# A decoder layer on one core: the o projection, its norms and the residual by rows of tokens

## The chip, the cores and the metric

The kernel runs on one core of a Trainium2 chip, in one launch. The metric is the device time of an execution in microseconds. The kernel before takes 1654.36 us, the median of three runs (1653.92 to 1654.64). Engines: PE is TensorE (PEld its weight loads), DVE is VectorE, ACT is ScalarE, POOL is GpSimd, SP is SyncE, whose queue issues nearly all DMAs.

## The reference

One decoder layer in float32, width 1024, for a prompt of 1024 tokens and, with its own convolution state, for 8 single sample tokens. The part that matters here:

```
z  = rms_norm(x, mix_pre_g) @ w_in            # split into u, v, b, c, x_in, r_a, r_b
v  = layer_norm(gelu(v));  y_a = (gelu(u) * spatial_mix(v)) @ w_a_out
y_b = (b * short_conv(c * x_in)) @ w_b_out
h  = sigmoid(r_a) * y_a + sigmoid(r_b) * y_b
o  = h @ w_o
x1 = x + rms_norm(o, mix_post_g)
f  = (silu(n @ w_gate) * (n @ w_up)) @ w_down,  n = rms_norm(x1, ffn_pre_g)
y  = x1 + rms_norm(f, ffn_post_g)
```

rms_norm divides a token's row by the root of its mean square and multiplies with a gain per column. The FFN is 2816 wide.

## The kernel before

**Numbers and layout.** Each float32 operand is split into a rounded high part and the rest (hi, lo), and a product is three matmuls: hi hi, hi lo, lo hi (`three`, L379). Most of the kernel keeps activations turned: channels lie on the partitions, tokens along the free axis. The 1032 tokens are four chunks (b, gg) of 258: 256 of the prompt and 2 samples. A matmul then has a 128x128 block of weights as stationary operand and 258 tokens moving. `tp` holds the operand's eight slots, hi and lo; `g` a stage's result; `ring_hi`/`ring_lo` seven prepared weight pieces; `stage0`, `stage1` the weights as they were loaded, 1 MB each; `ps` the eight banks of PSUM. Weight block b is loaded by SP (`load`, L711), ScalarE writes its hi parts (`hi`, L1112), GpSimd subtracts for the lo parts (`rest`, L953). Most blocks use a scheme of seven products in place of eight, with sums of quarters of weights (`sums`) and of activations made by VectorE; `QORDER` lists the plain blocks that use eight (`half`, L470).

**Stage of v (L386 to L462).** Nine tiles of tokens, the 8 samples first. Rows are loaded (`x_load`), ScalarE squares them with a sum, VectorE makes the root in eleven small instructions (`rsqrt`, L1516) and scales. TensorE turns eight blocks of the normalised rows (`turn_norm`), and eight of the raw rows (`turn_raw`); ScalarE copies the raw ones out and stores them in `xt_dram` (`keep`, L1089). v itself is computed with tokens as stationary operand and 512 columns of w_v moving, 48 matmuls a tile (`v_tile`). The transposes of tile i+2 stand behind the matmuls of tile i.

**The o stage (L583 to L606, L1321 to L1342, L1935 to L1977).** For each chunk, eight blocks m of 128 output columns: 24 matmuls with w_o's 128x128 blocks stationary and the chunk's 258 tokens moving. ScalarE evicts with the gain (L1326) and squares (L1332), GpSimd adds the squares, and a matmul with ones sums them over the partitions (`norm_sum`, L572) so that every partition has each token's sum. VectorE makes the root over 128x258 and scales (`x1`), adds the residual `xts`, loaded from `xt_dram`; ScalarE squares, VectorE adds, ones sum again (`second_norm`), and `x1_norm` scales into `g`. x1 is stored in `x1_dram`. `f_split` (ACT) and `f_rest` (DVE) then make hi and lo in `tp`. The first blocks of gate and up (`B_F`, `B_UP0`) run as four half runs on one half of the tokens each, plain, so that they can begin when chunks 0 and 1 are there. The next block pair uses seven products and needs the quarters' sums (`ft_total`, `ft_rest`).

**The end (L641 to L693, L1487, L2178).** y is computed turned. For each of 18 units (128 tokens by 512 columns) TensorE turns four blocks of f and four of x1, ScalarE copies x1 out of PSUM, VectorE scales and adds (`y_unit`), and SP stores rows.

**Order.** Each engine's order is written out by hand; engines meet through semaphores. What stands behind a waiting instruction in an engine's queue waits with it. w_o is loaded in columns, 128 of them a piece (`o_load`).

Of the kernel before, what the change touches and what calls it, by code (L numbers as in the profile page):

```python
# [7 lines left out]
D = 1024  # L8
# [22 lines left out]
B_UP0 = B_F + 1  # L31
B_D = B_F + 2 * J
# [31 lines left out]
STAGE = [b % 2 if b <= B_F else (0 if b == B_UP0 else (b + 1) % 2) for b in range(B_END)]  # L64
# [14 lines left out]
def places(b):  # L79
    return [0, 1, 2, 3] if b in QORDER else list(range(7)) if B_UP0 < b < B_D else TURNED  # L80


def freed(b, pos):
    place = places(b)[pos]
    if b == B_F + 2:
        return used(B_F, place) if place < 4 else done(LAST_RUN[B_UP0], 3)
# [25 lines left out]
O_LOADS = [0, 2, 1, 3, 4, 6, 5, 7]  # L112
O_ORDER = [O_LOADS] * 3 + [[0, 2, 4, 6, 1, 3, 5, 7]]
O_SLOT = {1: 5, 3: 7, 5: 4, 7: 6}
O_RING = {2: 4, 4: 0, 6: 2}
PARTS = [slice(0, 3), slice(3, 6), slice(6, 8)]
P_POST, P_PRE, P_OUT, P_CONV, P_LN = 0, KT, 2 * KT, 3 * KT, 6 * KT
P_ROWS = 7 * KT

def build(nc, x_prompt, x_sample, state_conv, mix_pre_g, mix_post_g, w_in, sgu_ln_g, sgu_ln_b, w_s,  # L120
# [7 lines left out]
    xt_dram = nc.dram_tensor("xt_dram", [4, 128, KT, 256], f32, kind="Internal").ap()  # L128
    xs_dram = nc.dram_tensor("xs_dram", [128, 4, KT, 2], f32, kind="Internal").ap()
    x1_dram = nc.dram_tensor("x1_dram", [4, 128, KT, CS], f32, kind="Internal").ap()  # L130
# [6 lines left out]
    with ctx:  # L137
# [36 lines left out]
        xt_odd = at("xt_odd", stage_at[1], [128, KT, CS])  # L174
        q = at("q", q_at, [128, 4, 2, CS])
        xt_even = at("xt_even", q_at, [128, KT, CS])
        xts = [(xt_even, xt_odd)[c % 2] for c in range(4)]
        inv_early, work_early = (at(n, ring_at + (6 + 7 * i) * 2048, [128, CS]) for i, n in enumerate(("inv_early", "work_early")))
# [5 lines left out]
        x_norm = at("x_norm", ring_at + 4096 * 2, [128, D])  # L184
        x_save = at("x_save", ring_at + 4096 * 3, [128, D])
# [12 lines left out]
        xs_raw = at("xs_raw", g_at + KT * D * 4, [128, 4, KT, 2])  # L198
        tail_out = s_bc[0:(2 + NS) * KT, 1].rearrange("p a c -> p (a c)")[:, 0:128]
        o_sum, o_sq0, o_sq1, x1_sum, base_t, root = s_a[:, 0], s_a[:, 1], s_b[:, 0], s_b[:, 1], s_c[:, 0], s_c[:, 1]  # L200
        invs = [inv_early[:, :]] * 3 + [q[:, 2, 1]]
        works = [work_early[:, :]] * 3 + [q[:, 3, 1]]
# [6 lines left out]
        xs = at("xs", hist_at, [128, 4, KT, 2])  # L209
# [4 lines left out]
        x1_smp = at("x1_smp", tail_at, [128, KT, NS])  # L214
# [39 lines left out]
        def norm_bank(n, c):  # L254
            return 6 + n if c < 3 else (7, 5)[n]

        x1_late = [at(f"x1_late{n}", stage_at[1] + n * 4096, [128, D]) for n in range(2)]
        x1_rows = [piece(5, u // 2, u % 2) for u in range(4)] + [t[:, :] for t in x1_late] + [piece(6, part, 0) for part in range(2)]
        y_rows = [piece((4, 0, 1, 2)[u // 2], u % 2, 0) for u in range(8)] + [piece(7, 0, 0)]
# [7 lines left out]
        def y_banks(v):  # L267
            return (4, 2, 0)[v % 3], (5, 3, 1)[v % 3]
# [21 lines left out]
        def w_ring(b, pos, kp=MP):  # L290
            if b != B_UP0:
                hi, lo = ring_hi[:, places(b)[pos]], ring_lo[:, places(b)[pos]]
            elif pos < 3:
                hi, lo = ring_hi[:, 4 + pos], ring_lo[:, 4 + pos]
            else:
                hi, lo = (tp[:, 3, part, 0].rearrange("p k c -> p (k c)")[:, 0:512] for part in range(2))
            return tuple(w[:, 0:128 * kp].rearrange("p (k c) -> p k c", c=128) for w in (hi, lo))

        def raw_part(b, pos, kp=MP):
            n = STAGE[b]  # L300
            k_odd, m_odd = divmod(pos, 2)[::-1] if b in QORDER else {0: (0, 0), 2: (1, 0), 6: (1, 1)}[pos]
            return stage[n][:, k_odd:2 * kp:2, 128 * m_odd:128 * m_odd + 128]

# [21 lines left out]
        raw_turned, norm_turned = sem("raw_turned"), sem("norm_turned")  # L325
        raw_copied, xt_saved = sem("raw_copied"), sem("xt_saved")
# [7 lines left out]
        stage_in = [sem("stage_in0"), sem("stage_in1")]  # L334
        s_sum, w_hi, w_lo = sem("s_sum"), sem("w_hi"), sem("w_lo")
# [6 lines left out]
        xs_in, xs_spread, xs_saved = sem("xs_in"), sem("xs_spread"), sem("xs_saved")  # L342
# [17 lines left out]
        o_full, o_copied, o_acc = sem("o_full"), sem("o_copied"), sem("o_acc")  # L360
        n_sum, n_sqrt, n_base, inv_ready = sem("n_sum"), sem("n_sqrt"), sem("n_base"), sem("inv_ready")
        xt_in, x1_saved = [sem("xt_in0"), sem("xt_in1")], sem("x1_saved")
        x1_done, x1_sq, x1_total, x1n_ready = sem("x1_done"), sem("x1_sq"), sem("x1_total"), sem("x1n_ready")
# [5 lines left out]
        x1_in, y_turned, y_done = [sem("x1_in0"), sem("x1_in1")], sem("y_turned"), sem("y_done")  # L369
        y_out, y_packed, x_turned, x1_copied = sem("y_out"), sem("y_packed"), sem("x_turned"), sem("x1_copied")  # L370
# [7 lines left out]
        def _(pe):  # L378
# [7 lines left out]
            def turn_raw(i):  # L386
                rows = rows_of(V_TILES[i])
                pe.wait_ge(x_in[i % 2], 16 * (i // 2 + 1))
                if i:
                    pe.wait_ge(raw_copied, i)  # L390
                for k in range(KT):
                    ins = pe.transpose(ps[:, 4 + k // 4, 128 * (k % 4):128 * (k % 4) + rows],  # L392
                                       x_rows[i % 2][0:rows, 128 * k:128 * k + 128], ident[0:rows, 0:rows])
                ins.then_inc(raw_turned, 1)

            def turn_norm(i):
                rows = rows_of(V_TILES[i])
                pe.wait_ge(x_scaled, i + 1)
                if i:
                    pe.wait_ge(xn_lo_done, i)  # L400
                for k in range(KT):
                    ins = pe.transpose(ps[:, 6 + k // 4, 128 * (k % 4):128 * (k % 4) + rows],  # L402
                                       x_norm[0:rows, 128 * k:128 * k + 128], ident[0:rows, 0:rows])
                ins.then_inc(norm_turned, 1)

            def v_tile(i):
# [4 lines left out]
                for k in range(KT):  # L411
                    if i == 0:
                        if k == 3:
                            turn_norm(1)
                        pe.wait_ge(wv_lo, k + 1)
# [10 lines left out]
            def turn_consts():  # L426
                pe.wait_ge(raw_copied, 9)
                pe.wait_ge(xn_lo_done, 9)
                pe.wait_ge(row_in, 16 * 7)
# [142 lines left out]
            def norm_sum(n, c, what):  # L572
                pe.matmul(ps[:, norm_bank(n, c), 0:CS], ones[:, :], what, start=True, stop=True).then_inc(n_sum, 1)

            def first_norm(c):
                pe.wait_ge(o_acc, (KT - 1) * (c + 1))
                norm_sum(0, c, o_sum)

            def second_norm(c):
                pe.wait_ge(x1_total, c + 1)  # L580
                norm_sum(1, c, x1_sum)
# [1663 lines left out]
```

## Time and profile before

| | us |
|---|---|
| median of three runs | 1654.36 |
| the profiled execution | 1651.66 |
| its span | 1649.9 |
| TensorE busy in it | 1616.9 |
| VectorE busy | 991.3 |
| ScalarE busy | 549.2 |
| GpSimd busy | 682.4 |

The span is the time from the first to the last recorded event of the profiled execution; the rest of its 1651.66 us lies around it. Busy times overlap between engines. Matmuls are pipelined, so a record's length is more than the distance to the next one. A timeline row merges like instructions in a row (x8), and a bracket at its end says how long the engine stood idle before it and what ended that.

### The profile page before, as it was taken

The numbers are of one execution on the slowest core, as the hardware profiler recorded it, in microseconds if no ns is written. First come the engines' busy times: TensorE is split into PE (matmuls) and PEld (weight loads), VectorE is DVE, ScalarE is ACT, GpSimd is POOL, SyncE is SP. The second block draws the span as 40 slices with busy tenths as digits, with TensorE's granted clock in tenths as the row PEclk, the third lists the DMA queues.
The fourth block names the chain that finished last, engine by engine and source line by source line (L and its number), as shares of the span: only waits on it lengthen the run. The fifth ranks groups of instructions, "written<-read, shape, count | busy, mean of one in ns | idle before, by whom it ended". The sixth has DMA issues, their size and how long they took to land.

```text
span 1649.9 us, 31035 instructions
## 1 busy us (share of the span) xinstructions
PE 1616.9 (98%) x12966; PEld 1586.1 (96%) x12966; DVE 991.3 (60%) x1409; ACT 549.2 (33%) x864; POOL 682.4 (41%) x495
## 2 busy tenths in 40 slices
PE   8999999999999999999999899999999999999998
PEld 5889999999999999999999899999999999999998
DVE  7657667587583334224428986444444447595976
ACT  5322332222223334212243543322223234342544
POOL 1001444444444443323442435444444443555392
PEclk9999999999999999999999999999999999999999
DMA  6302011320313335522332323222222324333433
GB/s 236 126 28 77 27 52 33 97 78 33 97 59 104 104 109 187 174 94 74 90 90 81 124 79 103 78 78 77 78 78 77 97 72 142 100 126 102 130 103 129
DMA packets 148494, 157.75 MB, mean 96 GB/s; under 512 B 6076, under 2 KB 136004, under 8 KB 147844
## 3 DMA queue, kind: packets, MB, share of 16 engines
q1 hardware_dynamic: 139732, 151.51, 28.6%
q10 hardware_dynamic: 8624, 4.27, 0.9%
q8 instruction: 103, 1.69, 0.4%
q14 instruction: 35, 0.29, 0.1%
HBM read 118.70 MB, written 37.09 MB: 94 GB/s over the span
## 4 chain that ended last, share of the span: by engine, by line
PE 86%; DVE 8%; issue 2%; DMA 1%; ACT 1%; SPq 0%; POOL 0%; DVEq 0%; ACTq 0%
PE ps L383 84%; DVE tp L2036 1%; PE ps L466 1%; DVE tp_f L2046 1%; DVE tp L1969 1%; DVE g L1961 1%; DMA gv<-in_w_in 1%; DMA stage<-in_w_gate 0%; DVE tp L2003 0%; PE ps L402 0%; PE ps L667 0%; PE ps L392 0%; DMA tp_f<-hid_dram 0%; PE ps L673 0%; DVE g L1951 0%
## 5 line engine op out<-in xcount | busy, mean ns | idle before, releaser
L383 PE MATMUL ps<-tp,ring_hi 128*128 128x258 f32 x7676 | 1253.4, 284 | 13.3 <-DVE tp L2036 6.4
L383 PEld LDWEIGHTS ps<-tp,ring_hi 128*128 128x128 f32 x7676 | 1069.7, 190 | 15.2 <-issue 13.1
L383 PE MATMUL ps<-tp,ring_lo 128*128 128x258 f32 x3838 | 796.1, 283 | 0.0
L383 PEld LDWEIGHTS ps<-tp,ring_lo 128*128 128x128 f32 x3838 | 606.7, 191 | 0.0
L962 POOL TENSOR_TENSOR ring_lo<-stage,ring_hi 128x512 fp32r<-128x512 f32 (+1 forms) x212 | 317.6, 1504 | 600.9 <-ACT ring_hi L1128 600.7
L962 POOL TENSOR_TENSOR ring_lo<-ring_f,ring_hi 128x512 fp32r<-128x512 f32 (+1 forms) x204 | 294.9, 1458 | 237.2 <-DVE ring_f L1623 109.6
L1128 ACT ACTIVATE ring_hi<-ring_f 128x512 fp32r<-128x512 f32 (+1 forms) x204 | 127.4, 626 | 484.0 <-DVE ring_f L1623 169.7
L1128 ACT ACTIVATE ring_hi<-stage 128x512 fp32r<-128x512 f32 (+1 forms) x212 | 128.7, 618 | 203.9 <-PE ps L383 145.6
L1620 DVE TENSOR_TENSOR ring_f<-stage 128x512 f32<-128x512 f32 (+1 forms) x51 | 40.4, 793 | 186.4 <-PE ps L383 117.8
L383 PE MATMUL ps<-wv_hi_t,tp 128*128 128x512 f32 x256 | 71.8, 397 | 0.0
L1641 DVE TENSOR_TENSOR s_a<-ps,s_a 128x516 f32<-128x516 f32 (+1 forms) x52 | 35.6, 684 | 49.2 <-PE ps L383 48.1
L2036 DVE TENSOR_TENSOR tp<-tp_f,tp 128x2064 fp32r<-128x2064 f32 (+1 forms) x24 | 58.2, 2428 | 1.2 <-ACT tp L1395 1.2
L383 PEld LDWEIGHTS ps<-wv_hi_t,tp 128*128 128x128 f32 x256 | 47.5, 188 | 10.6
L383 PE MATMUL ps<-tp 128*128 128x258 f32 x432 | 56.1, 288 | 0.0
L1139 ACT ACTIVATE s_a<-ps 128x516 f32<-128x516 f32 (+1 forms) x52 | 30.7, 589 | 72.3 <-PE ps L383 57.1
L383 PEld LDWEIGHTS ps<-tp 128*128 128x128 f32 x432 | 54.2, 193 | 0.4
L1652 DVE TENSOR_TENSOR s_a<-ps,s_a 128x516 f32<-128x516 f32 (+1 forms) x52 | 35.5, 682 | 31.8 <-PE ps L383 31.6
L1628 DVE TENSOR_TENSOR ring_f<-stage,ring_f 128x512 f32<-128x512 f32 (+1 forms) x51 | 53.5, 1048 | 0.0
L1892 DVE TENSOR_TENSOR g<-ps,q 128x516 f32<-128x516 f32 x16 | 11.1, 695 | 68.9 <-PE ps L383 61.0
L1395 ACT ACTIVATE tp<-tp_f 128x2064 fp32r<-128x2064 f32 (+1 forms) x24 | 42.6, 1780 | 20.5 <-DMA tp_f<-hid_dram 19.1
L2068 DVE TENSOR_TENSOR hq<-hq,q 128x516 f32<-128x516 f32 x40 | 44.9, 1123 | 2.2
L1911 DVE TENSOR_TENSOR s_bc<-ps,q 128x516 f32<-128x516 f32 x16 | 11.1, 695 | 49.9 <-PE ps L383 47.0
(235 smaller groups left out, 1306.3 us busy)
## 6 DMA issues: line engine op xcount, KB each, us to landing
stage<-in_w_in SPq DMA_DIRECT2D x24, 1024.0 KB, 5.8
stage<-in_w_gate SPq DMA_DIRECT2D x11, 1024.0 KB, 6.0
stage<-in_w_up SPq DMA_DIRECT2D x11, 1024.0 KB, 5.4
hid_dram<-hq SPq DMA_DIRECT2D x40, 258.0 KB, 3.1
tp_f<-hid_dram SPq DMA_DIRECT2D x20, 516.0 KB, 5.1
stage<-in_w_down SPq DMA_DIRECT2D x8, 1024.0 KB, 5.7
ob_dram<-q SPq DMA_DIRECT2D x16, 258.0 KB, 2.9
ra_dram<-q SPq DMA_DIRECT2D x16, 258.0 KB, 2.1
```

The source lines that it names most:

```text
L383: ins = pe.matmul(o, w, xc, start=first and n == 0, stop=last and n == 2)
L466: ins = pe.matmul(ps[:, 2 * r + n // 4, 128 * (n % 4):128 * (n % 4) + 128], gv[:, n, 128 * m:128 * m + 128], ws_t[:, 128 * m:128 * m + 128 ...
L962: pool.tensor_tensor(lo, src, hi.bitcast(f32), SUB).then_inc(w_lo, 1)
L1128: act.activation(w_ring(b, p, kp)[0], src, ACT.Copy).then_inc(w_hi, 1)
L1139: act.activation(s_a[:, gs], reg(Z, gs), ACT.Copy).then_inc(s1_done, 1)
L1395: act.activation(slot(s, 0, both, ks), slot_f(2 if s == 7 else s, 1, both, ks), ACT.Copy).then_inc(t_hi, 1)
L1620: ins = dve.tensor_tensor(out, a21, a22, ADD)
L1628: ins = dve.tensor_tensor(out, a12, ring(ring_f, b, 3, kp), SUB)
L1641: dve.tensor_tensor(s_a[:, gs], reg(X, gs), s_a[:, gs], ADD).then_inc(u1_done, 1)
L1652: dve.tensor_tensor(s_a[:, gs], reg(Z, gs), s_a[:, gs], ADD).then_inc(u2_done, 1)
L2036: dve.tensor_tensor(slot(s, 1, both, ks), slot_f(2 if s == 7 else s, 1, both, ks), slot_v(s, 0, both, ks), SUB).then_inc(t_lo, 1)
L2068: dve.tensor_tensor(hq[:, n], hq[:, n], q[:, n], MUL).then_inc(hid_ready, 1)
```

## The change

In the stage of v the raw transposes, their copies and `xt_dram` go. x_norm has two buffers and the normalised rows of tile i+1 are turned in the middle of tile i's matmuls, in two pairs of banks in turn.

The o projection takes tokens as stationary operand: for each of nine tiles (128 tokens, or the 8 samples, packed by GpSimd into `smp_hi`/`smp_lo`) the product goes to two banks, with 512 columns of w_o's rows moving. w_o is loaded by rows. Tiles 0 and 1 run interleaved, row block by row block. Each token's sum of squares is then along the free axis: ScalarE squares with a sum, VectorE makes the root on one column and scales straight from PSUM into the one buffer `x1n_rows`, adds the residual rows `res` (loaded from the input, two buffers), ScalarE squares again, VectorE scales into `x1n_rows`, TensorE turns eight blocks, ScalarE copies them to `g` (`x1n_keep`). x1 is stored by rows.

The first gate and up blocks get homes of their own in `tp` (`RAW_SLOT`), loaded after the last residual rows. At the end x1 is loaded straight into `y_rows`; a unit is four transposes of f, and every third unit is scaled by ScalarE and added by GpSimd.

```diff
+O_TILES = [2, 3, 8, 0, 1, 6, 7, 4, 5]
+O_BANK = [4, 2, 0] * 3
 # TensorE, stage of v
-            turn_raw(0)
             turn_norm(0)
-            turn_raw(1)
             for i in range(9):
-                v_tile(i)
-                if i + 2 < 9:
-                    turn_raw(i + 2)
-                    turn_norm(i + 2)
+                v_tile(i)              # turn_norm(i + 1) at its k == 4 (3 where i == 0)
 # TensorE, o stage
+            def o_part(i, j, k):
+                t, (a, kp) = O_TILES[i], (k % 2, k // 2)
+                if i < 2:
+                    pe.wait_ge(o_lo, j + 1)
...
+                outs = [ps[0:rows_of(t), O_BANK[i] + n, :] for n in range(2)]
+                w_h, w_l = ([w[:, 512 * n:512 * n + 512] for n in range(2)] for w in (w_o_hi[k], w_o_lo[k]))
+                ins = three(outs, x_h, x_l, w_h, w_l, j == 0, j == KT - 1)
+            def turn_x1n(i):
+                pe.wait_ge(x1n_ready, i + 1)
+                if i:
+                    pe.wait_ge(x1n_kept, i)
+                for k in range(KT):
+                    ins = pe.transpose(ps[:, x1n_banks(i)[k // 4], ...], x1n_rows[...], ident[...])
+                ins.then_inc(x1n_turned, 1)
+            for j, k in enumerate(O_LOADS):
+                o_part(0, j, k)
+                o_part(1, j, k)
+            for i in range(2, 9):
+                if i == 2:
+                    pe.wait_ge(o_packed, 8)
...
+                if i >= 3:
+                    pe.wait_ge(o_scaled, i - 2)
+                for j, k in enumerate(O_LOADS):
+                    o_part(i, j, k)
+                    if j == (KT - 1 if i == 2 else KT - 3):
+                        turn_x1n(i - 2)
+            turn_x1n(7)
             for i in range(4):         # gate on the first half of the tokens
...
                 half(r, i, PLAIN_BANK[i], lambda q: (f_lo, (3, 1, 4, 2)[q]))
+            turn_x1n(8)
 # VectorE
+            def x1(i):
...
+                y = o_root(i, i, o_sq)
+                if i == 0:
+                    dve.wait_ge(post_in, 16)
+                else:
+                    dve.wait_ge(x1n_turned, i)
+                dve.scalar_tensor_tensor(normed, o_rows, y, post_gain[0:rows], MUL, MUL).then_inc(o_scaled, 1)
+                dve.wait_ge(o_scaled, i + 1)
+                dve.wait_ge(res_in[i % 2], 16 * (i // 2 + 1))
+                dve.tensor_tensor(res[i % 2][0:rows, :], res[i % 2][0:rows, :], x1n_rows[0:rows, :], ADD).then_inc(x1_done, 1)
+            def x1_norm(i):
...
+                y = o_root(i, 9 + i, x1_sq)
+                dve.scalar_tensor_tensor(dst, src, y, pre2_gain[0:rows], MUL, MUL).then_inc(x1n_ready, 1)
+            for i in range(9):
+                x1(i)
+                if i == 5:
+                    f_rest(0)
+                elif i == 7:
+                    f_rest(1)
+                x1_norm(i)
 # ScalarE, from the seventh tile on (x1_square, x1n_keep and o_square before it likewise)
+            o_square(7)
+            prepare(B_F)
+            x1_square(7)
+            x1n_keep(6)
+            o_square(8)
+            x1n_keep(7)
+            prepare(B_UP0, 0, 3)
+            f_split(2)
+            x1_square(8)
+            silu_plain(r, 0)
 # SP
+            for i in range(7):
+                x1_save(i)
+                res_load(i + 2)
             load(B_F)
             load(B_UP0)
+            x1_save(7)
             load(B_F + 2)
+            x1_save(8)
 # GpSimd, behind w_o's low parts and the packing of the samples
-            (spread_samples, add_square and rest(B_F, ...) in turn)
+            prepare(B_F)
             prepare(B_UP0)
 # The end: y_bank(v) = (4, 2, 0, 5, 3, 1)[v % 6]; v % 3 == 0 on ScalarE and GpSimd
+            for v in range(18):        # VectorE
+                if v == 7:
+                    y_root_of(1)
+                    y_root_of(2)
+                if v % 3:
+                    y_unit(v)
```

## Rows read from the trace of the kernel before

**Rows 1.** The page: span, busy time, the chain's shares by engine.
```profile
span 1649.9 us, 31035 instructions
...
PE 1616.9 (98%) x12966; PEld 1586.1 (96%) x12966; DVE 991.3 (60%) x1409; ACT 549.2 (33%) x864; POOL 682.4 (41%) x495
...
PE 86%; DVE 8%; issue 2%; DMA 1%; ACT 1%; SPq 0%; POOL 0%; DVEq 0%; ACTq 0%
```

**Rows 2.** TensorE's waits: who waited for whom: total us, times, longest.
```profile
PE ps L573 <- DVE s_bc L1953: 5.0, 4, 3.3
...
PE ps L402 <- DVE x_norm L1530: 5.0, 2, 3.4
```

**Rows 3.** The chain in order of time: start us, length us, what.
```profile
40.62 11.09 PE ps L383 x48
...
51.71 0.87 PE ps L392 x8
...
211.11 277.75 PE ps L383 x2304
```

**Rows 4.** Timeline, all engines, 0 to 30: start, length, engine, line, idle before.
```profile
13.57 1.00 PE L383 MATMUL ps<-wv_lo_t,smp_hi 128*8 128x512 f32 x2
...
22.08 1.22 DVE L1542 TENSOR_TENSOR tp<-ps,tp 128x1024 fp32r<-128x1024 f32 x1
...
23.22 0.14 DVE L1527 TENSOR_SCALAR small<-small 128x1 f32<-128x1 f32 x1
...
23.59 0.63 PE L383 MATMUL ps<-wv_hi_t,smp_lo 128*8 128x512 f32 x2
...
25.33 1.28 DVE L1530 SCALAR_TENSOR_TENSOR x_norm<-x_rows,small,pre_gain 128x1024 f32<-128x1024 f32 x1
...
27.51 0.71 PE L383 MATMUL ps<-wv_hi_t,tp 128*128 128x512 f32 x2
```

**Rows 5.** Timeline 100 to 145, and a group of the page.
```profile
120.14 5.04 POOL L962 TENSOR_TENSOR ring_lo<-stage,ring_hi 128x512 fp32r<-128x512 f32 x4 [87.08 <-ACT ring_hi L1128]
...
121.49 1.21 DVE L1519 TENSOR_TENSOR small<-small 128x1 f32<-128x1 f32 x1
...
L1892 DVE TENSOR_TENSOR g<-ps,q 128x516 f32<-128x516 f32 x16 | 11.1, 695 | 68.9 <-PE ps L383 61.0
```

**Rows 6.** TensorE's timeline from 815 to 1003.
```profile
826.08 3.15 PE L383 MATMUL ps<-tp,stage_r 128*128 128x258 f32 x24 [1.09 <-POOL tp L973]
...
922.25 1.21 PE L573 MATMUL ps<-s_bc,ones 128*128 128x258 f32 x2 [3.30 <-DVE s_bc L1953]
...
922.90 4.48 PE L383 MATMUL ps<-tp 128*128 128x258 f32 x24
...
978.34 0.64 PE L383 MATMUL ps<-tp,ring_hi 128*128 128x258 f32 x4
...
994.80 0.72 PE L383 MATMUL ps<-tp,ring_hi 128*128 128x258 f32 x4 [1.82 <-DVE q L1635]
```

**Rows 7.** Timelines: ScalarE at 52, VectorE in the o stage.
```profile
52.67 1.02 ACT L1105 ACTIVATE x_save<-ps 128x1024 f32<-128x1024 f32 x1
...
922.12 3.88 DVE L1969 TENSOR_TENSOR tp<-g,tp 128x1032 fp32r<-128x1032 f32 x2
...
948.04 2.37 DVE L1969 TENSOR_TENSOR tp<-g,tp 128x1032 fp32r<-128x1032 f32 x2
```

**Rows 8.** The chain at 905; DMA issues: KB each, median us to landing.
```profile
905.54 8.08 DMA stage<-in_w_gate
...
stage<-in_w_gate SPq DMA_DIRECT2D x11, 1024.0 KB, 6.0
```

**Rows 9.** The end: VectorE's and GpSimd's timelines, then the last stretch by engine.
```profile
1635.69 11.61 DVE L2183 SCALAR_TENSOR_TENSOR tp_f<-ps,small,tp_f 128x512 f32<-128x512 f32 x14
...
1630.86 0.19 POOL L1039 COPY sum_smp<-q 128x8 f32<-128x8 f32 x1
...
1645.00:1649.90 4.90, 1.32 (x13) 1.08 (x10) 2.06 (x3) 1.20 (x2) 0.00 (x0) 0.94 0.74 293
```

More of the change, by code:

```diff
@@ L252, in ysq @@
             return q[:, 2 + n]
[L254 to L259, printed above, removed]
+        x1_late = [at(f"x1_late{n}", stage_at[0] + n * 4096, [128, D]) for n in range(2)]
+        y_rows = [piece(5, u // 2, u % 2) for u in range(4)] + [t[:, :] for t in x1_late] \
+            + [piece(6, part, 0) for part in range(2)] + [piece(7, 0, 0)]
         SAMPLES = 8
@@ L1148, in _ @@
                 wv_split(k)
-            keep(1)
+            norm_split(1)
+            square(2)
             for i in range(9):
+                if 0 < i < 8:
+                    norm_split(i + 1)
                 if 0 < i < 7:
@@ new lines, in x1n_keep @@
+            def x1n_keep(i):
+                t = O_TILES[i]
+                act.wait_ge(x1n_turned, i + 1)
+                first, second = x1n_banks(i)
+                if t == 8:
+                    rows = bank_pair(first, NS).rearrange("p k (g b i) -> p b g k i", g=2, b=2)
+                    for b in range(2):
+                        for gg in range(2):
+                            ins = act.activation(g[:, :, b, gg, 256:CS], rows[:, b, gg], ACT.Copy)
+                else:
+                    b, gg, off = home(t)
+                    dst = g[:, :, b, gg, off:off + 128]
+                    if second == first + 1:
+                        ins = act.activation(dst, bank_pair(first), ACT.Copy)
+                    else:
+                        for n, bank in enumerate((first, second)):
+                            ins = act.activation(dst[:, 4 * n:4 * n + 4], ps[:, bank, :].rearrange("p (k c) -> p k c", c=128), ACT.Copy)
+                ins.then_inc(x1n_kept, 1)
@@ L1955, in x1_norm, with o_root @@
-            def x1_norm(c):
-                b, gg = O_CHUNKS[c]
-                dve.tensor_copy(x1_smp[:, :, 4 * gg + 2 * b:4 * gg + 2 * b + 2], xts[c][:, :, 256:CS])
-                o_rsqrt(1, c)
-                for h in PARTS:
-                    for m in range(h.start, h.stop):
-                        ins = dve.scalar_tensor_tensor(g[:, m, b, gg], xts[c][:, m], par[:, P_PRE + m:P_PRE + m + 1], invs[c], MUL, MUL)
-                    ins.then_inc(x1n_ready, 1)
+            def o_root(i, col, ready):
+                rows = rows_of(O_TILES[i])
+                a, y, w = (small[0:rows, 20 + n:21 + n] for n in range(3))
+                dve.wait_ge(ready, i + 1)
+                link(dve.tensor_scalar(a, small[0:rows, col:col + 1], 1.0 / D, EPS, MUL, ADD))
+                rsqrt(y, a, w)
+                return y
@@ L1964, in f_rest @@
+            def x1_norm(i):
+                rows = rows_of(O_TILES[i])
+                quarters = (t[0:rows, :].rearrange("p (n c) -> p n c", n=4) for t in (x1n_rows, res[i % 2]))
+                dst, src = quarters
+                y = o_root(i, 9 + i, x1_sq)
+                if i == 0:
+                    dve.wait_ge(pre2_in, 16)
+                dve.scalar_tensor_tensor(dst, src, y, pre2_gain[0:rows], MUL, MUL).then_inc(x1n_ready, 1)
             def f_rest(c):
```

590 lines of the change are left out of this document (241 added, 349 removed).

## The prediction

> **What bounds the kernel now.** I began with the page: TensorE is busy 98% of the span, its chain share is 86%, and no other engine is above 60% [rows 1]. So a change counts by three things: TensorE work added or removed, waits opened or closed, and what lies behind the last matmul. The waits come next [rows 2]: little idle time, much of it before the sums over partitions that the change removes. Then the shapes. A tile of v, 48 matmuls of 512 columns, takes 11.09 us in the chain, 0.231 us each, and eight transposes take 0.87 us; 2304 matmuls of 258 columns take 277.75 us, 0.1206 each [rows 3]. I then read three places as timelines: the start [rows 4], the o stage [rows 6], and the end [rows 9].
>
> The sum is made against the profiled execution: 1651.66 us, 1649.9 of it span. The median of the runs is 2.7 us higher, at 1654.36; the time that I give is the difference added to that median.
>
> **Stage of v: raw transposes and their copies go.** TensorE first. Each tile of tokens loses one group of eight transposes. Before the second tile TensorE now stands until the rows for the third are normalised (VectorE 25.33 to 26.61) and starts its matmuls at 27.51, though the first tile ended at 24.0 (23.59 and two matmuls) [rows 4]. In the new order these transposes lie in the middle of the second tile, 5.5 us after its start, and their rows are ready by then. The tile itself can start at 24.0, since the low part of its own rows is there at 23.3 (22.08 and 1.22) [rows 4]. That is 3.5 us earlier, and the third tile's own transposes (0.87) are paid inside: 2.6. Six more tiles lose 0.87 each, 5.2. Together **-7.8**. What is late next? Per tile VectorE has 2.1 us of a norm's root (23.22 to 25.33), 1.3 of scaling, 1.2 of low part and some 4.6 of layer norm, 9.3 in all, under a new period of 11.1 + 0.87 = 12.0; so TensorE still sets the pace. Removed ScalarE copies, stores of xt, and SP's wait on the raw transposes cost nothing now, being beside matmuls. Less activity at the very start may leave the first tile longer at the lower clock (1.2 GHz: two 512-column matmuls last 1.00 there against 0.71 later [rows 4]), but its last part waits for loads anyway: 0 to +0.8. Bounds: -8.3 to -7.0.
>
> **o projection: TensorE work.** Removed: 768 matmuls at 0.1206 = 92.6, and 8 sums over partitions, 16 matmul records of 258 columns, 1.9. Added: 8 tiles of 48 matmuls of 512 columns, and the ninth, 8 samples as stationary operand, which costs as much as a full tile, as two such matmuls in the stage of v (0.63) do beside two of a full tile (0.71) [rows 4]: 9 x 11.09 = 99.8. Transposes of the normalised rows: 8 x 0.87 and a small one, 7.5. The four half runs of gate and up that follow, 384 matmuls, are 46.2 in both. Work after: 99.8 + 7.5 + 46.2 = 153.5. The same stretch of before lasts from 826.08 to 978.34, 152.3 with its waits, and the first up-weighted product after it has one more wait of 1.8, behind a crowded VectorE [rows 6]: 154.1. So if no wait were left, the stage would be level: -0.6. All that the transposes saved there would be the waits.
>
> **o projection: the waits that come.** The first two tiles run interleaved with the arriving rows of w_o, 2.8 us a row block against 2.4 of GpSimd for its low part, as now. From the third on, a tile's chain runs: turn of the tile before ends (x1n_rows is one buffer), scale from PSUM 1.3, add 1.2 (as the 128x1024 low part), square on ScalarE 1.1 (its 128x1024 copy is 1.02), root 2.1, scale 1.3, turn [rows 4, 7]: 7.4 with hand-overs, 8.6 in the turn where two f_rest lie beside the square. The turns are 12.0 apart, so this is hidden by 2 us or more, about 1 at the first two.
>
> The last full tile is different. Its turn is issued right behind the ninth tile's matmuls, only 2.8 us after the turn before. Against that stand: scale to 1.4, add to 2.6, two f_rest (2.4 free, 3.9 beside GpSimd [rows 7]) to 6.4; ScalarE meanwhile has the four gate-weight copies, queued ahead of the square, which end about 5 (the load, 6.0 us [rows 8], is issued after the last residual load), so the square ends about 6.4 too; root 2.1 to 8.5; scale 1.3 to 9.8; hand-over 0.1. With free ports TensorE waits 9.9 - 2.8 = 7.1. But GpSimd then subtracts the four gate weights. Beside just such a block of four (5.04 us) the small VectorE instructions of a root took 1.21 us each instead of 0.19 pitch, four in the block, of which one stands in the rows [rows 5]. Instructions with an operand in PSUM keep their time: 695 ns mean for 516 columns [rows 5]. I take it that two of this root's eleven are caught, +2.0, and 0.2 for the square: wait **9.3**, bounds 7.1 and 12.
>
> The Trainium skill has a rule here, in "SBUF — State Buffer", section "SBUF: two separate sides": a VectorE instruction with two SBUF inputs and a GpSimd one exclude each other for the whole instruction. By that rule every one of the eleven root instructions could wait a full GpSimd one until the four are done, some 5 us and not 2.2; the wait would be 12, the end of my bound.
>
> Then the clock. After 3.30 idle at 922.25 the granted clock shows the lower level, and 24 matmuls span 4.48 against 2.9 to 3.0 warm: 1.5 lost [rows 6]. After a longer wait I take 2.0, bounds 1.5 and 3.4. Behind the wait all is covered: the ninth turn lies after 11.6 us of gate products, while its chain (scale, add, square behind f_split, root, scale) is some 9 to 10; up's first half hides the last f_rest. The sums of quarters for the first seven-product run are finished before the last half run, so the 1.8 of before should not return. SP's order (saves, residual loads, then weights) has 3 to 5 us to spare at each tile. Stage: -0.6 + 9.3 + 2.0 = **+10.7**, bounds +8.0 and +14.8.
>
> **The end.** Now every unit of 512 columns is eight transposes, 0.87 us, and VectorE's 14 last units take 11.61 (1635.69 to 1647.30) [rows 9]. After: four transposes a unit, every third unit on ScalarE and GpSimd, two of three on VectorE at 0.75 (PSUM operand, so not slowed). The first units can be scaled from about 1629.2 as before the samples' sum. GpSimd starts its adds at 1631.05; VectorE does four units to 1632.2, then both roots, partly beside two adds, to 1635.5; eight units at 0.75 to 1641.5; GpSimd's last four adds at 1.3 from 1635.5 end 1640.7. Computing thus ends 5.8 earlier. But three output tiles, 1.5 MB, become ready within the last 1.5 us; the last stretch shows 293 GB/s at a share of 0.74 [rows 9], 396 at full share, so 4 us of transfer plus 1.8 fixed: end at about 1645.5. **-4.5**, bounds -6.0 and -2.5.
>
> Elsewhere (u to gates, the other up and gate products, down) the edits only rename slots and stages: 0, within 0.5.
>
> **Sum.** -7.8 + 10.7 - 4.5 = -1.6: 1650.1 for the profiled execution, **1652.8** on the median.
>
> **Rivals.** Bound between "same" and the others is 0.2%, 3.3 us, about what a measurement can tell: below 1651.1 faster, above 1657.7 slower.
> First, the turn's wait is short: roots escape GpSimd, idle costs little clock (7.1 + 1.5 - 0.6 = 8.0), and the last stores are not held by transfer (-5.8): -7.8 + 8.0 - 5.8 = -5.6, 1648.8. For it: the 695 ns of PSUM instructions, and that the weights' block may start after the root. Against: f_rest at 3.88 beside GpSimd [rows 7], in this very stretch. With the wait of the turn gone wholly it would be near 1642.
> Second, slower: the gate weights land late. Gate and up are issued back to back, 2 MB; if their packets share the engines, gate lands after 12 us and not 6. Its four copies stand in ScalarE's queue ahead of the square of the last tile, so the square, root and turn slip by 6: wait 15.3, clock 3: stage +17.7, sum -7.8 + 17.7 - 4.5 = +5.4, 1659.8. It decides from a landing about 7 us after issue. For: 8.08 us at 905.54, behind another megabyte. Against: the median of 6.0 [rows 8], and that nothing large is issued ahead of gate here.
> Third, the shapes do not do what I read: rows of w_o as 512-column operand from the ring cost more than w_v's, or the single buffer of rows makes a wait in each of six tiles of 1 us or more. Then +6 and up, 1659 or more. Little speaks for it: 0.231 holds for all v tiles, the 8-row one too.
>
> **Numbers.** Forecast and its neighbourhood within 0.2%: 0.45. First rival with what lies beyond: 0.36. Second: 0.12, third: 0.07. Range: 8 in 10 from 1646.5 to 1659.0, which holds the bounds of the three parts taken mostly together (all low -6.3, all high +5.3). Faster 0.36, same 0.45, slower 0.19.
>
> **What would show it.** Second tile of v starts near 24.0 and tiles come every 12.0; the o stage has nine blocks of 11.1; one TensorE wait of 7 to 12 us before the transposes of the last full tile, on VectorE's scaling, with half clock behind it; no wait of 1.8 in the first seven-product run; last transposes near 1640 in old time. Wrong if waits stand at several turns, if that one is under 5, or if the end gains less than 2.5.

## The result: 2.6 us slower, 0.15%

Over 20 executions each the changed kernel takes 1654.97 us in the median (1652.88 to 1657.45), the kernel before 1652.36 (1651.57 to 1654.66): ratio 1.0015, 95% interval 1.0008 to 1.0021. The forecast was a difference of -1.6 us, 1652.8; the three runs that its base was taken from stood 2.0 us above the median of the twenty. The profiled execution of the changed kernel took 1653.63 us, 1651.8 of it span. Its page, line by line against [rows 1]:

```profile
span 1651.8 us, 30181 instructions
...
PE 1611.5 (98%) x12542; PEld 1557.3 (94%) x12542; DVE 971.5 (59%) x1512; ACT 524.8 (32%) x801; POOL 661.0 (40%) x477
...
q8 instruction: 100, 1.64, 0.4%
```

TensorE's waits (who waited for whom: total us, times, longest), against [rows 2]. The waits before the sums over partitions, 5.0 us in four, are gone; one of 9.4 has come. Two small ones on VectorE's `q`, at 489 and 423, were not there before:

```profile
PE ps L584 <- DVE x1n_rows L1937: 9.4, 1, 9.4
PE ps L397 <- DVE x_norm L1521: 7.4, 1, 7.4
PE ps L388 <- DVE tp L2009: 7.4, 3, 3.4
...
PE ps L553 <- DVE q L1647: 1.3, 1, 1.3
```

Both kernels cut at the same points of the program (end of the v stage, first product of the o stage, the first product after the first wait of the down stage, that after the third, end). First before, then after; columns: stretch, its length, busy time of each engine with its instructions, granted clock, DMA share, GB/s:

```profile
0.00:198.65 198.65, 188.97 (x1170) 162.59 (x1170) 137.72 (x315) 66.85 (x89) 30.88 (x31) 1.00 0.30 97
198.65:826.08 627.43, 626.19 (x5193) 625.83 (x5194) 331.11 (x481) 172.51 (x276) 265.87 (x185) 1.00 0.29 93
826.08:1395.89 569.81, 559.38 (x4601) 557.05 (x4601) 330.59 (x411) 197.44 (x336) 252.02 (x189) 1.00 0.29 91
1395.89:1552.17 156.28, 151.48 (x1243) 151.13 (x1243) 117.82 (x107) 60.40 (x74) 75.34 (x49) 0.99 0.38 121
1552.17:1649.90 97.73, 90.89 (x762) 89.49 (x762) 74.04 (x98) 52.04 (x91) 58.34 (x42) 1.00 0.31 98
```

```profile
0.00:190.49 190.49, 180.10 (x1098) 153.84 (x1098) 138.17 (x315) 60.04 (x79) 30.74 (x31) 1.00 0.24 79
190.49:820.29 629.80, 626.68 (x5193) 625.96 (x5194) 329.65 (x481) 172.43 (x276) 264.63 (x185) 1.00 0.29 93
820.29:1401.45 581.16, 569.54 (x4320) 544.62 (x4321) 315.74 (x520) 186.27 (x295) 224.08 (x165) 0.99 0.28 90
1401.45:1558.36 156.91, 151.71 (x1242) 151.18 (x1243) 117.95 (x107) 60.25 (x74) 75.73 (x49) 0.99 0.38 120
1558.36:1651.80 93.44, 83.47 (x690) 81.69 (x690) 69.95 (x92) 45.78 (x79) 65.80 (x48) 0.99 0.27 103
```

Read by differences: -8.16 in the v stage, **+2.37 in a stretch with the same 5193 matmuls in both**, +11.35 from the o stage to the first wait of down (0.61 of it that wait: 2.24 for 1.63), +0.63 within down, -4.29 at the end. Together +1.9, as the spans.

The one large wait is the forecast's, link by link. The chain of the changed kernel (start us, length, what):

```profile
923.10 0.89 PE ps L584 x8
...
924.09 1.29 DVE x1n_rows L1925
...
925.41 1.22 DVE res L1928
926.63 3.36 DVE tp L1944 x2
...
930.28 0.89 DVE small L1510
...
931.20 1.20 DVE small L1511
...
934.80 1.30 DVE x1n_rows L1937
...
936.14 1.97 PE ps L584 x8
```

TensorE was through with the ninth tile at 926.8 and stood until 936.1. The turn then took 1.97 us instead of 0.87, at the lower clock.

### The profile page after: what moved, and what is told of

Same layout as the page of the kernel before. It is cut to its first block, busy times and chain, and to the rows that moved or that the text cites. A ratio compares the mean times of both kernels' runs of the same rounds, so it can differ in the third digit from the quotient of the medians.

```text
span 1651.8 us, 30181 instructions
## 1 busy us (share of the span) xinstructions
PE 1611.5 (98%) x12542; PEld 1557.3 (94%) x12542; DVE 971.5 (59%) x1512; ACT 524.8 (32%) x801; POOL 661.0 (40%) x477
## 4 chain that ended last, share of the span: by engine, by line
PE 90%; DVE 5%; issue 2%; DMA 1%; ACT 0%; POOL 0%; DVEq 0%; SPq 0%; POOLq 0%; ACTq 0%
PE ps L388 88%; DVE tp L2009 1%; PE ps L455 1%; DVE tp_f L2019 1%; PE ps L584 1%; DMA stage<-in_w_down 0%; DMA stage<-in_w_in 0%; PE ps L397 0%; DMA tp_f<-hid_dram 0%; ACT tp L1381 0%; DVE g L2102 0%; DVE tp L1944 0%; DVE tp_f L2158 0%; POOL ring_lo L959 0%; DVE s_a L1642 0%
## 5 line engine op out<-in xcount | busy, mean ns | idle before, releaser
L388 PE MATMUL ps<-tp,ring_hi 128*128 128x258 f32 x7388 | 1200.0, 284 | 11.3 <-DVE tp L2009 7.4
L388 PEld LDWEIGHTS ps<-tp,ring_hi 128*128 128x128 f32 x7388 | 1024.8, 190 | 12.7 <-issue 12.7
L388 PE MATMUL ps<-tp,ring_lo 128*128 128x258 f32 x3694 | 755.2, 283 | 0.0
L388 PEld LDWEIGHTS ps<-tp,ring_lo 128*128 128x128 f32 x3694 | 579.4, 191 | 0.0
L959 POOL TENSOR_TENSOR ring_lo<-stage,ring_hi 128x512 fp32r<-128x512 f32 (+1 forms) x205 | 304.4, 1492 | 570.2 <-ACT ring_hi L1088 570.1
L1088 ACT ACTIVATE ring_hi<-stage 128x512 fp32r<-128x512 f32 (+1 forms) x205 | 124.5, 617 | 199.3 <-PE ps L388 139.6
L388 PE MATMUL ps<-tp 128*128 128x512 f32 (+1 forms) x384 | 72.0, 340 | 0.0
L388 PEld LDWEIGHTS ps<-tp 128*128 128x128 f32 x384 | 59.7, 191 | 8.5
L959 POOL TENSOR_TENSOR tp<-tp_f,tp 128x512 fp32r<-128x512 f32 x4 | 6.5, 1645 | 94.2 <-ACT tp L1088 94.2
```

The source lines that it names most:

```text
L388: ins = pe.matmul(o, w, xc, start=first and n == 0, stop=last and n == 2)
L959: pool.tensor_tensor(lo, src, hi.bitcast(f32), SUB).then_inc(w_lo, 1)
L1088: act.activation(w_ring(b, p, kp)[0], src, ACT.Copy).then_inc(w_hi, 1)
```

## Experiments

Times are medians in us; the ratio is to the kernel before on the same chip in the same job, with its 95% interval. The kernel before took 1653.96 us in the job of e1 to e4, 1653.33 in that of e5 to e8, 1653.12 for e9 to e11 and 1653.22 for e12 to e14, so times of different jobs are compared by their ratios. The last five columns are the stretches above in us, each from one profiled execution:

```
                              time     ratio   interval          to end v  same work  o to down  down    end
before                        1652.36  1                         198.65    627.43     569.81     156.28  97.73
after                         1654.97  1.0015  1.0008 to 1.0021  190.49    629.80     581.16     156.91  93.44
e1 rest early                 1655.07  1.0005  0.9996 to 1.0014  191.16    630.10     581.12     156.88  93.94
e2 e1 + two row buffers       1646.47  0.9956  0.9944 to 0.9968  191.71    629.26     572.90     155.20  93.63
e3 v stage only               1649.98  0.9976  0.9964 to 0.9987  191.22    630.02     572.48     156.47  97.81
e4 end only                   1648.43  0.9965  0.9953 to 0.9977  198.61    628.08     569.85     156.04  93.12
e5 e2 + square first          1647.10  0.9962  0.9950 to 0.9975  191.02    629.20     573.42     156.60  93.86
e6 e1 + square first          1654.75  1.0009  1.0000 to 1.0018  191.45    629.08     581.58     158.33  93.56
e7 e3 + 128 waits on TensorE  1654.31  1.0011  1.0002 to 1.0021  197.04    627.58     572.03     155.12  97.83
e8 e5 + 128 waits             1652.35  0.9992  0.9984 to 1.0001  198.69    628.01     574.96     156.20  93.64
e9 e5 + GpSimd later          1651.72  0.9992  0.9983 to 1.0000  190.62    630.20     577.34     157.36  93.78
e10 e6 + GpSimd later         1656.43  1.0024  1.0015 to 1.0033  190.77    630.80     581.51     158.66  93.56
e11 e9 + 54 small turns       1648.45  0.9973  0.9964 to 0.9982  191.36    627.48     576.44     156.25  93.57
e12 e11 + GpSimd twice later  1644.71  0.9950  0.9936 to 0.9965  191.29    627.56     573.32     156.16  93.87
e13 before + 51 small turns   1658.86  1.0035  1.0022 to 1.0048  199.51    629.55     572.21     157.68  98.85
e14 e3 + 54 small turns       1648.67  0.9972  0.9959 to 0.9984  191.37    627.98     571.74     158.82  98.79
```

### The parts alone: e3 and e4

e3 is the kernel before with `turn_raw` and `keep` gone, two homes for `x_norm`, and the v stage's order of the changed kernel; e4 is the kernel before with the changed end. Both leave out part of what the layer computes: e3 reads its residual from other elements of the input, e4 adds x where x1 belongs, with the same number of bytes. e7 and e14 below are built on e3.

```diff
+                sp.dma_start(xts[c][:, :, 0:256], x_prompt[0, 256 * (2 * b + gg):256 * (2 * b + gg) + 256, :]
+                             .rearrange("(p r) (j c) -> p (r j) c", r=2, c=256))
...
+                    dst, src = y_rows[u], x_prompt[0, 256 * (2 * gg + b) + cols.start:...]
```

> The kernel before with the v stage of the changed one alone: no raw rows turned, copied or saved; the residual of the o stage is loaded with the same number of bytes from other elements of the input (so the residual is left out of what is computed). Theory V (8.1 us gained in the v stage and kept): 1643.9 to 1644.9, that is 7.5 to 8.5 us under the kernel before. Rival L (the earlier v stage makes loads of the next stages land late for TensorE, as the two waits of 0.6 and 1.3 us in the changed kernel's profile at 423 and 489 us): 5.0 to 6.5 us under it, with these two waits in its profile.

> The kernel before with the end of the changed one alone: no turns of the residual, a third of the units scaled by ScalarE and added by GpSimd; the residual added is x instead of x1 (same bytes, from the input). Theory E (the end gains 4.3 us as the two profiles stand to each other, and nothing else moves): 1647.6 to 1648.6, that is 3.8 to 4.8 us under the kernel before. Rival D (the end gains 4.3 us but the new end's loads, or other chances of transfers, cost the 1.3 us that the down stage lost in the changed kernel): 2.5 to 3.5 us under it, with waits of over 2 and over 3.4 us in the down stage.

e3: rival L, and more. The v stage ends 7.4 us earlier, but the kernel gains only 4.0 (0.24%, interval 0.13 to 0.36%). Both waits are there:

```profile
PE ps L549 <- DVE q L1616: 1.3, 1, 1.3
PE ps L384 <- DVE q L1594: 0.9, 2, 0.7
```

So they came with the v stage, not with the o stage. Then 2.7 us more went between 821 and the down stage, of which 0.8 is a longer first wait of down and most of the rest lower clock (last section). e4: 5.8 us under before by the ratio (0.35%, interval 0.23 to 0.47%), 5.5 by the medians, 4.6 of them in the end stretch of its profile; theory E, a little above it. The only loss elsewhere is 0.65 us in the equal stretch, with a wait of 0.79 us at 495 that before's profile does not have, though TensorE's instructions up to there are the same in both: so much comes and goes between executions.

### The large wait, one arm at a time: e1, e6, e10, and with two buffers e2, e5, e9

```diff
 e1:             if i == 7: f_rest(1)      # before x1(i), was behind it
 e6 = e1 and     x1_square(7)              # before prepare(B_F) on ScalarE, was behind it
 e10 = e6 and    pool.wait_ge(x1n_ready, 8)  # before prepare(B_F) on GpSimd
 e2 = e1 and     x1n_rows in two homes by turns: sb_at, and q[:, :, 0, 0:256]
                 dve.wait_ge(x1n_turned, i - 1)   # was i
 e5 = e2 and     x1_square(7) first
 e9 = e5 and     pool.wait_ge(x1n_ready, 8)
```

> The changed kernel with the two subtractions of the second column block (VectorE, 3.4 us in all) set before the scaling of the eighth tile instead of between its two norms. Theory W (the 9.4 us wait of TensorE is the length of VectorE's chain after the turn of the seventh tile, 12.0 us from 924.1 to 936.1): the wait falls by 3.4 to 6.0 us, and some of the slow small operations beside GpSimd move too; 3.4 to 5 us faster than the changed kernel, so 1650.0 to 1651.6 on its median of 1654.97. Rival R (the chain is set by what GpSimd and the landing of the gate weights do at 925 to 934): the small operations wait on, the wait stays above 8 us, and the gain is under 1.5 us.

> As e1_rest_early, and the normed rows have two homes by turns (the second in the part of q that is free then), so that VectorE can scale a tile while TensorE still has to turn the one before. Theory W: the chain of the eighth tile starts some 9 us earlier, the wait of 9.4 us goes to under 2, the clock does not fall, and the kernel is 9 to 12 us faster than the changed one: 1643 to 1646, 0.4 to 0.6% under the kernel before. Rival R (something else than the one row buffer holds the tile back, VectorE's own 10 us of work per tile or the gate weights): a wait of 4 us or more stays before the turn of the eighth tile or at the first product of the gate stage, and the time is 1648 or more.

e1 missed: the wait went from 9.4 to 8.8 only. Rival R described it. The 3.4 us of subtractions were one of two arms side by side; the other was ScalarE, whose square stood behind the split of weights that landed late. VectorE's timeline of e1:

```profile
926.47 1.22 DVE L1928 TENSOR_TENSOR res<-res,x1n_rows 128x1024 f32<-128x1024 f32 x1
931.40 0.15 DVE L1912 TENSOR_SCALAR small<-small 128x1 f32<-128x1 f32 x1 [3.71 <-ACT g L1279]
```

e2 was right in kind and a little short of its numbers (1646.47 for 1643 to 1646, a wait of 2.3 us for under 2): no lower clock after the wait, and 8.2 us less than e1 from o to down. The second buffer without the early subtractions was not run.

> As e1_rest_early (one row buffer), and ScalarE squares the eighth tile's sum before it splits the gate weights. In e1 the two subtractions were gone from the chain, but VectorE then sat 3.7 us for that square, which stood behind weights that landed at 928.1; the wait only went from 9.4 to 8.8. If these are two arms of one wait, taking both away must shorten it by 3 us or more: a wait of 5 to 6.5 us, and 3 to 4.5 us less than the changed kernel, 1650.5 to 1652. If the one row buffer alone set the 9 us, it stays above 8 and the time within 1 us of the changed kernel's 1654.97.

> As e2_two_rows, and ScalarE squares the eighth tile's residual sum before it splits the gate weights instead of behind that (in e2 the square waited until 923.3, and VectorE 3.2 us for it). Theory S (the rest of the wait, 2.3 us before the turn at 929.8, is ScalarE's order): the turn waits under 0.5 us and the kernel is 1.5 to 2.5 us faster than e2_two_rows, 1644 to 1645. Rival G (the split gate weights are late then): a wait of 1 us or more appears before the first products of the gate stage, and the time stays within 1 us of e2_two_rows.

Both missed in the same way: 8.6 and 2.7 us of wait stayed although both arms were gone. GpSimd's four subtractions now started at once beside the root. VectorE's timeline of e5:

```profile
922.38 0.16 DVE L1514 SCALAR_TENSOR_TENSOR small<-small 128x1 f32<-128x1 f32 x1
922.57 1.13 DVE L1515 SCALAR_TENSOR_TENSOR small<-small 128x1 f32<-128x1 f32 x1
923.74 1.23 DVE L1513 TENSOR_TENSOR small<-small 128x1 f32<-128x1 f32 x1
925.01 1.21 DVE L1514 SCALAR_TENSOR_TENSOR small<-small 128x1 f32<-128x1 f32 x1
926.25 1.22 DVE L1515 SCALAR_TENSOR_TENSOR small<-small 128x1 f32<-128x1 f32 x1
927.50 0.16 DVE L1513 TENSOR_TENSOR small<-small 128x1 f32<-128x1 f32 x1
```

GpSimd worked from 922.38 to 927.45: four instructions, four small ones slowed, 4.1 us.

> As e6_rest_and_square_early (one row buffer), and GpSimd waits for the scaling of the eighth tile. In e6 the wait was 8.6 us, with four small operations at 1.12 to 1.21 us beside GpSimd. Theory P: the wait falls by 4.1 us to about 4.5 us, and the time by 3.5 to 5 us, to 1650 to 1651.5 (the changed kernel 1654.97). If the row buffer alone set it, 8.6 us stay. Rival Q as for e9: the subtractions, started 4 us later against their use, cost over 1.5 us at the first products of the gate stage.

> As e5_two_rows_square_first, and GpSimd starts its four subtractions of the gate weights (5.07 us) only when the eighth tile is scaled. Theory P (what is left of the wait is the slowing of VectorE beside GpSimd: in e5 four small operations of the chain took 1.13 to 1.23 us instead of 0.16 while GpSimd was at work from 922.4 to 927.5, 4.1 us in all): these four take 0.16 us each, the scaling ends at about 925, the wait of 2.7 us before the turn at 929.4 is gone, and the kernel is 2 to 3 us faster than e5's 1647.1. Rival Q (GpSimd's work is only moved in front of the gate stage): a wait of over 1.5 us before its first products, and no gain over 1 us.

The mechanism held to a tenth: e10's wait before the eighth tile's turn is 8.61 - 4.06 = 4.55, e9's is gone. The gain did not come: by the ratios e10 is 2.5 us slower than e6 and e9 5.0 slower than e5, where gains of 3.5 to 5 and of 2 to 3 were expected. GpSimd's block ran into the ninth tile's root instead, and that tile's turn waited 3.5 us in e10 and 3.8 in e9, after which the clock in e9 was at half for 5 us. In e9 (who waited for whom, 821 to 960):

```profile
PE ps L587 <- DVE x1n_even L1943: 3.8, 1, 3.8
```

So the 9.4 us are a chain with three movable arms (subtractions, ScalarE's order, GpSimd's block) on a single row buffer; taking arms away one by one gave nothing (from o to down 581.1 to 581.6 us in e1, e6 and e10), the second buffer gave 8.2 (e2 against e1, e5 against e6).

### The late loads: e7, e8, e11 to e14

What delays the unchanged stretch is one load of w_in. VectorE's timeline, first before, then after:

```profile
428.53 0.69 DVE L1620 TENSOR_TENSOR ring_f<-stage 128x512 f32<-128x512 f32 x1 [6.78 <-DMA stage<-in_w_in]
```

```profile
422.04 0.69 DVE L1610 TENSOR_TENSOR ring_f<-stage 128x512 f32<-128x512 f32 x1 [8.41 <-DMA stage<-in_w_in]
```

Issued at 422.34 and 414.21, it landed 6.1 and 7.7 us later. The transfers of the changed kernel from 419 to 421 show what is in it:

```profile
q1 hardware_dynamic: 688, 0.69, 101.5%
q8 instruction: 1, 0.02, 3.0%
```

One packet of 16 KB, for 3% of 16 engines in 2 us, that is 1 us of one engine. The page has 103 such packets before and 100 after:

```profile
q8 instruction: 103, 1.69, 0.4%
```

TensorE's 12966 matmuls and as many weight loads, with its waits, are some 26400 instructions, 256 for each of the 103 packets, and the changed kernel's 12542 by the same count some 25600 for its 100; in steady work they come 15.4 us apart (128 matmuls of 0.1206). The change takes 72 transposes, with their weight loads 144 instructions, out of the v stage, and so moves every later fetch against every later load. In before they fall at about 415 and 431, on both sides of this load, in after at 419.

The Trainium skill, "Perfetto Trace Analysis", section "The 4-stage abstract model", has an instruction at 64 bytes, by which 256 make the 16 KB; the trace agrees. The Trainium skill, "Trainium Architecture — The Big Picture", section "The software stack", has the instruction streams brought to the engines when the program is loaded; here that is not the whole of it: the 103 packets come all through the execution.

e7 and e8 add `pe.wait_ge(consts, 1)` 256 times ahead of TensorE's first work (128 instructions); e11 and e14 add 54 turns of 8 by 8 there, e13 adds 51 to the kernel before. From e11:

```diff
+            small_turns(44)      # e13: 10, 27 and 14 in its three gaps
             turn_norm(0)
+            small_turns(10)
```

> As e3_v_only, with 128 instructions more on TensorE (waits that are long met) in the time in which it stands before its first work. Theory F (TensorE's instructions come in blocks of 16 KB, one for 256 instructions, 15.4 us apart; 153 instructions fewer in the v stage moved one of these fetches into the load of w_in that lands at 423, which landed 1.6 us later for it): with 128 back, the fetch falls some 5 us before that load, its landing takes 6 to 7.5 us instead of 8.3, the wait of 0.7 us at 424 is gone and that of 1.35 us at 490 is under 0.9; 1.0 to 4 us less than e3_v_only's 1649.98. Rival J (these waits come with the time of day of the loads, whatever TensorE fetches): both waits stay, the landing stays over 8 us, the time within 0.7 us of e3_v_only.

> As e5_two_rows_square_first with the same 128 instructions more on TensorE at the start. Theory F: the waits of 0.4 us at 424 and 1.3 us at 490 go or shrink to under 0.9, and it is 1 to 3 us faster than e5; rival J: no difference over 0.7 us. As the fetches of all later stages move too, a wait that is new elsewhere (down stage) would speak for F as well, with the other sign.

In time both missed: each of these 128 instructions takes 0.11 us or a little more, TensorE's first work began at 14.96 instead of 7.6 and 7.8, and both kernels were 4 to 6 us slower in all, where 1 to 4 less was expected. The stretch of equal work is what they are read for: 627.58 after 630.02, 628.01 after 629.20, with no wait at 424, and this load and the one after it landing in 7.1 us in the median of the two in e7, 8.3 in e3.

> As e9_pool_waits, with 54 turns of 8 by 8 on TensorE (108 instructions) while it stands idle before its first work (44, 0.12 us each as the first turn's eight took 0.99 us, in the 5.6 us before it, and 10 in the 1.3 us behind it). This takes the place of e7's and e8's padding, which was too long and started TensorE 7.5 us late. Theory F (the phase of TensorE's instruction fetches): the fetch moves 6.5 us ahead, out of the load that lands at 423, and the waits of 0.5 us at 424 and 1.15 at 490 become 0 and under 0.7; from 191 to 820 it takes 627.6 to 628.3 us instead of e5's 629.2; the start costs nothing or, if TensorE's clock rises earlier by this work, gives up to 3 us. In all 1 to 4 us faster than e9. Rival J: the waits stay.

> As e3_v_only with the 54 small turns of e11_pool_waits_small_turns at the start. Theory F: no wait at 424, under 0.5 us at 490; 191 to 821 takes 627.3 to 628 us instead of 630.0; 1.5 to 3.5 us faster than e3_v_only's 1649.98, so 1646.5 to 1648.5. Rival J: 630 us again and no gain.

Without that cost: e11 3.3 us faster than e9, stretch 627.48 for 630.20; e14's stretch 627.98 for 630.02, with a wait of 0.71 us left at the second load where under 0.5 was expected. In the whole time e14 missed: 1.3 us less than e3 in the median where 1.5 to 3.5 was expected, 0.7 by the ratios, whose intervals overlap. In its profile the down stage and the end took 3.3 us more than in e3.

> The kernel before with 51 turns of 8 by 8 (102 instructions) on TensorE in its idle time before the v stage's products, and nothing else. Theory F (phase of TensorE's instruction fetches against the loads): in the kernel before they were asked for at about 415 and 431 and at 476 and 491, outside the loads of w_in that land at 428.5 and about 488; 102 instructions set them 6.1 us ahead, to about 425 and 485, into both. Waits then appear at about 430 and 495, as the changed kernel has them (0.3 to 1.3 us each), and the stretch from the bias turn's end at 198.7 to the o stage at 826.1 (627.4 us) grows by 1 to 2.7 us. Rival J (the waits come with the v stage's changed order): it stays at 627.2 to 627.8. At the start itself 0 to 3 us may be won by an earlier full clock or 0.8 lost; read this at the 198.7 mark.

Opposite sign, nothing else changed: before gets 5.6 us slower (0.35%, interval 0.22 to 0.48%). In the equal stretch it has the changed kernel's waits, 1.8 us together for none; the one expected at 430 did not come, both lie at the second load:

```profile
PE ps L571 <- DVE q L1664: 1.4, 1, 1.4
PE ps L383 <- DVE q L1642: 0.4, 1, 0.4
```

Its profiled execution lost 0.9 us at the start, 2.1 here, 2.4 up to the down stage, 1.4 in down and 1.1 at the end. The first two were forecast; the rest is the first wait of down (2.38 for 1.63) and longer stretches of the lower clock.

All sixteen profiles fall into two groups by this second load, the one issued between 475 and 485. Before, then after:

```profile
stage<-in_w_in SPq DMA_DIRECT2D x1, 1024.0 KB, 5.7
```

```profile
stage<-in_w_in SPq DMA_DIRECT2D x1, 1024.0 KB, 7.2
```

In nine profiles (after, e1, e2, e3, e5, e6, e9, e10, e13) a 16 KB packet starts while it is under way; it lands 6.7 to 7.5 us after issue, and the stretch of equal work takes 629.1 to 630.8 us. In the other seven (before, e4, e7, e8, e11, e12, e14) none does; it lands in 5.7 to 6.4 us and the stretch takes 627.4 to 628.1.

> As e11_pool_waits_small_turns, and GpSimd's subtractions for the first up weights (three of 1.27 us) wait until the ninth tile is scaled. In e9 and e11 the wait of the eighth tile was gone, but GpSimd's row of work then ran on to 934.7 and caught six small operations of the ninth tile's chain (0.79 to 1.23 us each instead of 0.16), and TensorE waited 3.75 us before that tile's turn. Theory P: two to three are caught now, the wait falls to 0.3 to 1.5 us, with less of the slower clock behind it; 2.5 to 5 us faster than e11's 1648.45, so 1643.5 to 1646. Rival U (the up weights are late): a wait of over 1.5 us before their first products, gain under 1.5 us.

e12 hit: 1644.71, 8.3 us (0.50%) under before and 10.7 under the changed kernel by the ratios. Its turns wait for nothing; 1.7 us of wait, 1.27 and 0.46, moved to the first products with the up weights (rival U in part). Against e2 GpSimd's two waits gained nothing (573.32 for 572.90 from o to down); what e12 has over e2 is the moved fetches, 1.7 us in the equal stretch. The whole times of the two do not differ clearly (0.9936 to 0.9965 and 0.9944 to 0.9968).

## Why the prediction was wrong

The measured time lies inside the stated range; the direction was wrong. Point by point, against its own steps:
- v stage, -7.8 within -8.3 and -7.0: measured -8.16 to its end. Right. Tile two starts at 23.64, forecast 24.0, and tiles come every 12.0.
- o stage, +10.7: measured 11.35 - 0.61 = +10.74. The wait, 9.3, is 9.38, in part by luck: three of the root's eleven small operations were caught beside GpSimd instead of two (2.8 us for 2.0), but the last subtraction before the root ended 6.0 us after the turn, not 6.4, and the 0.2 for the square was not needed. The clock was 1.1 in the turn and 0.3 behind it, 1.4 for 2.0; the full tiles take 11.16 for 11.09, +0.6. No wait of 1.8 in the first seven-product run, as forecast. The second rival did not come: ScalarE had the gate weights at 926.4 and its four copies ended 4.6 us after the turn, forecast 5.
- The end, -4.5: measured -4.29, and -4.6 alone in e4. Here two misses cancel: the last computing ended at 1646.7, 6.8 us earlier than before's 1647.3 counted from the start of the end stretch (forecast 5.8), and from there to the end it took 5.1 us where before took 2.6 (2.5 more, forecast 1.3).
- **The step that failed is the short one: "the edits only rename slots and stages: 0, within 0.5".** In the profiled executions these stages lost 2.37 + 0.61 + 0.63 = 3.6 us, which is the whole of the miss there (forecast -1.6, span +1.9). The 2.37 is 1.96 of waits behind two late loads and 0.4 around them, the 0.61 the first wait of down. I priced stages whose code did not change at nothing, though the change takes instructions out of the stream ahead of them. e3, e7, e11, e13 and e14 show the 2.4 in both directions: the loads of w_in with the least slack land 1 to 2 us later when a fetch of TensorE's instructions falls into them. For the 0.61 and the 0.63 the cause stays open.
- The three priced terms measured -8.16 + 10.74 - 4.29 = -1.7, so the sign hung on that zero. Half of the v stage's gain never reached the end (e3: 7.4 to 4.0).
- The remaining 0.7 between -1.6 + 3.5 and the +2.6 of the medians is that the changed kernel's profiled execution lies 1.3 us under its median, that of before 0.7 under its own.

Open: why the first wait of down is 1.63 us in before and e4 and 2.1 to 2.7 in every other kernel, also in those whose fetches of TensorE were moved back; the other engines' fetches (35 and 36 small packets) move too, and no run separates them. And how the packet delays a load: the two loads landed in 8.2, 8.3 and 8.8 us (medians) with it in the first of them in after, e3 and e1, in 6.7, 7.2 and 7.1 without it in before, e4 and e7, but in 7.2 in e13, which has one there too. What the runs show is that the number of TensorE's instructions ahead decides whether the wait at the second load is 1.2 to 1.4 us long (nine profiles) or 0 to 0.8 (seven); that the packet holds up one of the 16 engines is read from the records and not tested alone.

## What to carry to other kernels

A stage with unchanged code is not at zero when instructions are taken out or put in ahead of it: in this kernel 102 idle instructions cost 5.6 us and 108 in another variant gained 3.3 (e13, e11), but in a third the whole gain was not clear of noise (e14). That is more than many edits are worth, so price it by the slack of the loads there, and test a gain with the stream padded by some 100 instructions in idle time. When a wait has several arms of one length, shortening one gives nothing (e1, e6); look for the resource that starts the chain late, here the single row buffer. Work moved off one chain lands on the next: GpSimd's block cost 4 us and more beside the ninth tile's root as it had beside the eighth's.

## What the runs showed of the hardware that was not expected

- TensorE's instructions arrive in packets of 16 KB for 256 instructions during the execution, about 1 us of one DMA engine each, and where they fall against the loads is set by the count of instructions ahead.
- Beside each GpSimd subtraction of 1.25 us one VectorE operation on a single column lasted up to 1.1 to 1.2 us instead of 0.16, four for the four in e5; one that was caught midway took less (0.88 in the changed kernel). With GpSimd silent each of the eleven in e9 took 0.15 or 0.16.
- The lower clock follows short waits at one time and not at another, and their length does not tell which. Behind the same wait before the first seven-product run, before (1.82 us) had 42 matmuls in 5 us at full clock, e3 (1.86) 29 at 0.66:

```profile
994.80:999.80 5.00, 5.00 (x42) 5.00 (x43) 4.93 (x7) 1.70 (x4) 2.96 (x3) 1.00 0.64 205
```

```profile
990.31:995.31 5.00, 5.00 (x29) 5.00 (x30) 4.93 (x7) 1.71 (x4) 2.96 (x3) 0.66 0.69 207
```

But e4, with 1.86 us, had 42 at full clock as well, and e13, with 1.82, had 29 at 0.66. The 13 matmuls fewer are 1.6 us. Executions of one kernel lie 3 to 5 us apart, and their mean granted clock goes with that: in the job of e13 the kernel before took 1651.8 to 1652.1 us in the three at 0.998 and 1654.3 to 1654.5 in the two at 0.996.
